# Causal attention loops: the first turned head of a pair right behind the value products, its copy ahead of the next exponentials

## The reference

```
even layer (here "fox", 8 heads):
    s = q k^T / 8 + (F_query - F_key)       # forget gate
    s = where(key <= query, s, -inf);  p = softmax(s);  o = p v
    beside it: a gated linear attention in chunks of 64 (here "GLA")
odd layer (here "odd", 16 heads):
    the top-k keys of an index score are kept; s = q k^T / 8 + bias(distance)
    s = where(kept and key <= query, s, -inf);  p = softmax(s);  o = p v
```

## Time and profile before

| | |
|---|---|
| median of 3 runs | 1404.54 us (1402.19 to 1405.95) |
| the profiled execution's own time | 1404.41 us |
| its span, first to last instruction | 1402.4 us |
| mean granted clock of TensorE, share of full speed | 0.993 |
| TensorE busy | 1361.1 us (97%) |
| VectorE, ScalarE, GpSimd busy | 971.0, 677.5, 72.4 us |
| fox loop, about | 631 to 672 us |
| odd loop, about | 1136 to 1194 us |

### The profile page before, as it was taken

How to read it: one execution, slowest core, us unless ns; L and a number is a source line. 1 busy time by engine, 2 the same in 40 slices (tenths; PEclk the granted TensorE clock), 3 DMA queues, 4 the chain that set the end, 5 groups by cost and what they waited for, 6 DMA issues and landing times.

```text
span 1402.4 us, 19395 instructions
## 1 busy us (share of the span) xinstructions
PE 1361.1 (97%) x7680; PEld 1156.9 (82%) x7680; DVE 971.0 (69%) x1321; ACT 677.5 (48%) x1056; POOL 72.4 (5%) x112
## 2 busy tenths in 40 slices
PE   8999999999999999998999999999999988999997
PEld 6888988888888888897888888888888866888886
DVE  5786776666687667657577667777666677576764
ACT  5576454443565444455554444444445455444442
POOL 0300010000000000003000000000000043000000
PEclk9999999999999999999999999999999999999999
DMA  8433556555446555454346555465554543465550
GB/s 301 156 125 121 180 173 219 180 184 191 165 155 217 190 195 176 160 177 147 122 150 216 196 188 180 157 204 186 191 187 148 163 137 88 150 210 189 181 191 34
DMA packets 67594, 241.31 MB, mean 172 GB/s; under 512 B 7999, under 2 KB 8392, under 8 KB 67504
## 3 DMA queue, kind: packets, MB, share of 16 engines
q1 hardware_dynamic: 65200, 234.19, 50.4%
q0 software_dynamic: 2016, 5.77, 1.6%
q10 hardware_dynamic: 288, 0.11, 0.0%
HBM read 238.88 MB, written 1.09 MB: 171 GB/s over the span
## 4 chain that ended last, share of the span: by engine, by line
PE 72%; issue 14%; DVE 6%; ACT 3%; DMA 2%; POOL 1%; DVEq 0%; POOLq 0%; ACTq 0%; SPq 0%
PE pp L455 71%; DVE wlo L1626 2%; PE pp L464 2%; DMA raw<-w_chunks 1%; ACT whi L1192 1%; DVE hx L1634 1%; DVE fa L1626 1%; ACT pbuf L1339 1%; DMA gns<-gains 0%; ACT hx L1193 0%; POOL fa L2346 0%; DVE fa L2173 0%; ACT xn L1231 0%; DVE fa L1634 0%; ACT fa L1193 0%
## 5 line engine op out<-in xcount | busy, mean ns | idle before, releaser
L455 PE MATMUL pp<-hx,whi 128*128 128x512 f32 (+1 forms) x2400 | 728.9, 365 | 6.0 <-DVE hx L1634 3.0
L1626 DVE TENSOR_TENSOR wlo<-raw,whi 128x1024 fp32r<-128x1024 f32 (+1 forms) x445 | 522.7, 1214 | 152.6 <-ACT whi L1192 152.3
L455 PE MATMUL pp<-hx,wlo 128*128 128x256 f32 x2032 | 569.3, 280 | 0.0
L455 PEld LDWEIGHTS pp<-hx,whi 128*128 128x128 f32 x2400 | 428.0, 189 | 89.0 <-issue 7.5
L1192 ACT ACTIVATE whi<-raw 128x1024 fp32r<-128x1024 f32 (+1 forms) x445 | 442.4, 1041 | 104.4 <-PE pp L455 93.6
L455 PEld LDWEIGHTS pp<-hx,wlo 128*128 128x128 f32 x2032 | 384.7, 189 | 2.1
L455 PE MATMUL pp<-whi,ra 128*128 128x512 f32 x1144 | 371.1, 395 | 0.0
L455 PEld LDWEIGHTS pp<-whi,ra 128*128 128x128 f32 x1144 | 215.2, 188 | 50.1 <-issue 0.9
L455 PE MATMUL pp<-wlo,ra 128*128 128x512 f32 x572 | 225.1, 394 | 0.0
L1706 DVE TENSOR_REDUCE fa<-pp 128x512 f32<-128x1024 f32 x104 | 126.9, 1220 | 80.8 <-PE pp L455 80.8
L1192 ACT ACTIVATE ra<-fa 128x512 fp32r<-128x512 f32 x63 | 39.8, 632 | 229.8 <-DVE fa L1634 229.8
(11 more groups left out here) (172 smaller groups left out, 775.4 us busy)
## 6 DMA issues: line engine op xcount, KB each, us to landing
raw<-w_chunks SPq DMA_DIRECT2D x437, 512.0 KB, 5.1
fa<-t_rows POOLq DMA_DIRECT2D x16, 128.0 KB, 3.4
raw<-w_chunks SPq DMA_DIRECT2D x5, 256.0 KB, 5.7
fx<-x_t SPq DMA_DIRECT2D x2, 512.0 KB, 5.1
X<-x_in SPq DMA_DIRECT2D x2, 512.0 KB, 9.2
fa<-g_fin POOLq DMA_DIRECT2D x2, 512.0 KB, 4.5
fa<-f_rows POOLq DMA_DIRECT2D x8, 128.0 KB, 3.2
out_dram<-X SPq DMA_DIRECT2D x2, 512.0 KB, 2.7
```

What stands on the lines that cost most here:

```text
L455: return pe.matmul(o, lhs, rhs, start=first, stop=last, skip_group_check=True)
L1626: return dve.tensor_tensor(o, a, b, op)
```

## The change

In the causal blocks, and only there, four orders are changed; every operation stays, and none is added.

- TensorE turns the first head of pair p-1 right behind the value products, ahead of `extra` and `fill(p, 0)`.
- ScalarE goes: copy of the first turned head, exponentials of the first head of pair p, copy of the second turned head, exponentials of the second head, the high part of pair p-2, `evict` of (p, 0), one split, `evict` of (p, 1) and (p, 2), one split. Where there is no pair p left, the split of (p, 0) stands between the two copies.
- VectorE takes the low part of pair p-2 and `evict` of (p, 0) behind the scaling of pair p, and `evict` of (p, 1) ahead of `lows(p, 0)`. Where there is no pair p left, `lows(p, 0)` stands ahead of `evict` of (p, 0).
- The rest is the same code put into functions (`high`, `low`, `exponentials`, `turned_copy`).

```diff
--- before.py
+++ after.py
@@ -686,12 +686,15 @@
                         weigh(2 * pr + 1, 0)
                         weigh(2 * pr, 1).then_inc(s_pv)
                         weigh(2 * pr + 1, 1).then_inc(s_pv)
+                    if causal and 1 <= p <= pairs:
+                        turn_weights(2 * p - 2)
                     point[0] = (p, 0)
                     extra(p)
                     fill(p, 0)
                     ended[name, p, 0] = consumed[0]
                     if 1 <= p <= pairs:
-                        turn_weights(2 * p - 2)
+                        if not causal:
+                            turn_weights(2 * p - 2)
                         fill(p, 1)
                         turn_weights(2 * p - 1)
                         fill(p, 2)
@@ -1317,37 +1320,61 @@
                         split_half()
                     split_at[name, p, at] = next_half[0]
 
+                def high(pr):
+                    act.wait_ge(s_pv, h0 + 2 * pr + 2)
+                    copy(out_hi(name, pr), ps[obk[pr % len(obk)]][:, 0:256]).then_inc(s_ohs)
+
+                def exponentials(h):
+                    hc = h0 + h
+                    nm, sm, rs = head_stats(hc)
+                    src = stt[:, h % 2, 0:tot] if causal else ps[sbk[h % 2]][:, 0:tot]
+                    if causal:
+                        act.wait_ge(s_smax, 2 * (hc - 16) + 2)
+                    else:
+                        act.wait_ge(s_negm, hc + 1)
+                    if h >= 4:
+                        act.wait_ge(s_ptn, hc - 3)
+                    if h >= 8:
+                        act.wait_ge(s_shr, hc - 7)
+                    o = weights_slot(name, h)
+                    for t in range(2):
+                        y = act.activation(o[:, off[t]:off[t] + kl[t]], src[:, off[t]:off[t] + kl[t]], ACT.Exp,
+                                           bias=nm[:, t:t + 1], scale=-1.0 if causal else 1.0, accum_out=sm[:, t:t + 1])
+                    y.then_inc(s_ex)
+
+                def turned_copy(h):
+                    act.wait_ge(s_ptn, h0 + h + 1)
+                    if h >= 2:
+                        act.wait_ge(s_pv, h0 + h - 1)
+                    copy(ptb[:, h % 2, 0:tot], ps[tbk[h % len(tbk)]][:, 0:tot]).then_inc(s_ptc)
+
                 for p in range(pairs + 2):
+                    if causal:
+                        for par in range(2):
+                            if 1 <= p <= pairs:
+                                turned_copy(2 * p - 2 + par)
+                            if p < pairs:
+                                exponentials(2 * p + par)
+                            elif par == 0:
+                                one_more(p, 0)
+                        if p >= 2:
+                            high(p - 2)
+                        evict((name, p, 0))
+                        if p < pairs:
+                            one_more(p, 0)
+                        evict((name, p, 1))
+                        evict((name, p, 2))
+                        one_more(p, 1)
+                        continue
                     if p >= 2:
-                        pr = p - 2
-                        act.wait_ge(s_pv, h0 + 2 * pr + 2)
-                        copy(out_hi(name, pr), ps[obk[pr % len(obk)]][:, 0:256]).then_inc(s_ohs)
+                        high(p - 2)
                     for h in (2 * p, 2 * p + 1) if p < pairs else ():
-                        hc = h0 + h
-                        nm, sm, rs = head_stats(hc)
-                        src = stt[:, h % 2, 0:tot] if causal else ps[sbk[h % 2]][:, 0:tot]
-                        if causal:
-                            act.wait_ge(s_smax, 2 * (hc - 16) + 2)
-                        else:
-                            act.wait_ge(s_negm, hc + 1)
-                        if h >= 4:
-                            act.wait_ge(s_ptn, hc - 3)
-                        if h >= 8:
-                            act.wait_ge(s_shr, hc - 7)
-                        o = weights_slot(name, h)
-                        for t in range(2):
-                            y = act.activation(o[:, off[t]:off[t] + kl[t]], src[:, off[t]:off[t] + kl[t]], ACT.Exp,
-                                               bias=nm[:, t:t + 1], scale=-1.0 if causal else 1.0, accum_out=sm[:, t:t + 1])
-                        y.then_inc(s_ex)
+                        exponentials(h)
                     evict((name, p, 0))
                     one_more(p, 0)
                     if 1 <= p <= pairs:
                         for par in range(2):
-                            h = 2 * p - 2 + par
-                            act.wait_ge(s_ptn, h0 + h + 1)
-                            if h >= 2:
-                                act.wait_ge(s_pv, h0 + h - 1)
-                            copy(ptb[:, par, 0:tot], ps[tbk[h % len(tbk)]][:, 0:tot]).then_inc(s_ptc)
+                            turned_copy(2 * p - 2 + par)
                             evict((name, p, 1 + par))
                     one_more(p, 1)
 
@@ -1798,6 +1825,11 @@
                     while next_half[0] < split_at.get((name, p, at), 0):
                         split_half()
 
+                def low(pr):
+                    dve.wait_ge(s_ohs, h0 // 2 + pr + 1)
+                    tt(out_lo(name, pr), ps[obk[pr % len(obk)]][:, 0:256], out_hi(name, pr).bitcast(F),
+                       ALU.subtract).then_inc(s_ols)
+
                 for p in range(pairs + 2):
                     for h in (2 * p, 2 * p + 1) if p < pairs else ():
                         hc = h0 + h
@@ -1820,13 +1852,11 @@
                                 dve.wait_ge(s_ex, hc - 7)
                             dve.tensor_reduce(nm, bank[:, 0:tot].rearrange("p (t k) -> p t k", t=2), AX.X, ALU.max,
                                               negate=True).then_inc(s_negm)
-                    if p >= 2:
-                        pr = p - 2
-                        dve.wait_ge(s_ohs, h0 // 2 + pr + 1)
-                        tt(out_lo(name, pr), ps[obk[pr % len(obk)]][:, 0:256], out_hi(name, pr).bitcast(F),
-                           ALU.subtract).then_inc(s_ols)
+                    if p >= 2 and not causal:
+                        low(p - 2)
                     lows(p - 1, 1)
-                    evict((name, p, 0))
+                    if not causal:
+                        evict((name, p, 0))
                     for h in (2 * p, 2 * p + 1) if p < pairs else ():
                         hc = h0 + h
                         nm, sm, rs = head_stats(hc)
@@ -1838,8 +1868,16 @@
                             sl = slice(off[t], off[t] + kl[t])
                             y = ts(o[:, sl], o[:, sl], rs[:, t:t + 1], None, ALU.mult, None)
                         y.then_inc(s_shr)
+                    if causal:
+                        if p >= pairs:
+                            lows(p, 0)
+                        evict((name, p, 0))
+                        evict((name, p, 1))
+                        if p >= 2:
+                            low(p - 2)
                     lows(p, 0)
-                    evict((name, p, 1))
+                    if not causal:
+                        evict((name, p, 1))
                     evict((name, p, 2))
```

## The result

| | before | changed kernel |
|---|---|---|
| median | 1405.24 us (1402.19 to 1406.85, 4 runs) | 1419.3 us (1417.31 to 1421.4, 4 runs) |
| ratio | | 1.0101 [1.0088, 1.0114] |
| profiled execution's span | 1402.4 us | 1419.4 us |
| fox, first scores to last value products | 39.04 us | 54.66 us |
| odd, the same | 55.36 us | 57.54 us |

The kernel is 1.0% slower, 14.1 us in the medians and 17.0 us in the two profiled spans. The profiled execution of the changed kernel is the slowest of its four (1421.4 us), that of the kernel before lies 0.8 us under its median, so sizes read from this pair of traces are on the high side. The 17.0 us by place: fox +15.6, odd +2.2, the stretches ahead of, between and behind the loops -0.8 together (the last one, from the last value products of odd to the end, took 210.75 against 210.74 us and takes nothing up).

The account below looks back on a forecast made before the run. TensorE, busy 97% of a 1402.4 us span, was taken as the bound. Fox +8.2 and odd +1.1 gave a span of 1411.7, and 2.0 more for the execution gave 1413.7 us; range 1406 to 1420.

Parts of the forecast that it names:

- What bounds the kernel, and that a loop's delay reaches its end: Whole kernel: TensorE busy 97% of 1402.4 us; delay at a loop's last value products reaches the end whole.
- The stall before go1: Fox, p = 4: the split ahead of the states makes TensorE wait 5.6 us; go1 starts 5.3 us later.
- Fox, p = 3: Fox up to p = 3: eviction and low behind the scaling delay the next value products by 1.65 us.
- the term taken at nothing: Both loops: VectorE's scalings meeting GpSimd's masks in the new order, bounded at -2 to +2 us, taken as 0.
- one fall of 1.8 among four places: Four short stalls, two in fox and two in odd: one clock fall of 1.8 us counted, booked on odd.
- Value products of p = 4 to go0's end: Fox, p = 4: value products, turn, extra(4) and three units take 4.15 us to go0's end.
- go1 to the last value products: Fox, end of the loop: this stretch takes 5.2 us instead of 4.06, +1.1.
- Odd: Odd loop: 0.7 us of gain left, one clock fall of 1.8 us, together +1.1 us.
- one fall behind the 5.6 us stall: Fox, behind the wait before go1: TensorE's clock falls once, +1.8 us.
- the rival with falls at all four short stalls: Fox and odd: three more clock falls of 1.8 us than counted, 1419.1 us; chance 0.12.
- the clock holds over short stalls: Fox and odd: only the 5.6 us stall brings a clock fall, +7.5 us, 1411.9 us; chance 0.12.
- Low is in time: Odd: VectorE does low before TensorE's next scores end, so the change wins, 1396 us; chance 0.09.

Follow-up runs that it names:

- e8: Kernel before, with only the split of (p, 0) put ahead of evict(p, 0) where no pair is left, on ScalarE and VectorE; 1409.81 us, ratio 1.0035.
- e9: Changed kernel plus unread identity products (9, 4, 11 and 23) filling TensorE's four stalls in fox; 1414.66 us, ratio 1.0059.
- e11: e4 with VectorE's low part behind both scalings in fox alone; 1398.64 us, ratio 0.9939.
- e7: e4 with the second turned head's copy put between the two exponentials; 1403.89 us, ratio 0.9992.
- e4: Changed kernel with only first turn and first copy early; second copy back behind exponentials and split, VectorE as before; 1397.4 us, ratio 0.9950.
- e10: e4's order in odd alone, fox as in the kernel before; 1399.03 us, ratio 0.9947.
- e6: e4 with VectorE's low part behind both scalings; 1398.48 us, ratio 0.9951.

## Why the prediction was right or wrong, point by point

The time, 1419.3, lies in the range given, 5.6 us above the forecast and 0.7 below the range's upper end. The direction and the mechanism came as forecast, the size did not: 9.2 us of loss were forecast and 14.1 measured. Span against span the forecast is 7.7 us too low: 7.4 in fox, 1.1 in odd, and 0.8 the other way in the other stretches. By its steps:

- *What bounds the kernel, and that a loop's delay reaches its end: right.* Nothing behind a loop took anything up (210.75 against 210.74 us).
- *The stall before go1: right to the tenth.* 5.6 forecast, 5.63 measured, with ScalarE's split ahead of the states as the rows above show; e8 has the same 5.6 in the old kernel.
- *Fox, p = 3: too small by 4.0.* Forecast +1.65 at p = 4's value products, measured +5.6. 1.1 of it is VectorE: extra(3) started at 653.43, and the loop had begun 0.98 us earlier than before, so that this stands against the forecast's 653.3 as 654.4. VectorE took 11.74 us before from its mask at 640.40 to kg's eviction at 652.14, and 12.64 us in the changed kernel (639.36 to 652.00), with the same instructions. So 0.9 of the 1.1 is the term taken at nothing, how VectorE meets GpSimd's masks; here are VectorE's and GpSimd's rows of the changed kernel:

```profile
644.47 2.10 DVE L1653 TENSOR_TENSOR wlo<-raw,whi 128x1024 fp32r<-128x1024 f32 x1
...
647.60 1.22 DVE L1653 TENSOR_TENSOR wlo<-raw,whi 128x1024 fp32r<-128x1024 f32 x1
...
648.93 1.03 DVE L1657 TENSOR_SCALAR pbuf<-pbuf,st 128x128 f32<-128x128 f32 x2
```

```profile
644.30 0.48 POOL L2349 TENSOR_TENSOR fa<-fa,cst 128x128 f32<-128x128 f32 x1
644.72 0.75 POOL L2350 TENSOR_TENSOR fa<-fa,cst 128x256 f32<-128x256 f32 x1
...
647.63 1.50 POOL L2349 TENSOR_TENSOR fa<-fa,cst 128x128 f32<-128x128 f32 x1 [2.15 <-DMA fa<-f_rows]
```

  A split of 1.22 us took 2.10 beside a mask, a mask of 0.48 us took 1.50 where a split had begun 0.03 us before it. The other 2.9 is the low clock over extra(3) and five units (from extra(3) to the next value products 11.54 us, against 8.71 in e9), where the forecast had one fall of 1.8 among four places.
- *Value products of p = 4 to go0's end: too small by 3.0.* 7.2 instead of 4.15, the second fall (extra(4) 3.70 instead of 1.99, units 0.64 instead of 0.36). The order of the work was right.
- *go1 to the last value products:* 7.4 against 5.2 and the counted 1.8, 0.4 too little.
- *Odd: about right, for partly wrong reasons.* Forecast +1.1, measured +2.2. The cycles measured 7.4, 5.6, 7.1, 6.4, 6.4 and 5.2 against 6.0, 5.3, 7.2, 6.4, 6.4 and 5.2. p = 3's value products came 1.2 late. The first cycle was 1.4 longer: the clock fell behind its wait as forecast (1.55 us for the eight products), but cost more than the 0.7 given to it there. The further fall of 1.8 that was counted did not come: the clock held over 2.45 and 1.96 us.

So the term that was mis-sized is the clock in fox. The prediction counted 1.8 us there, for one fall behind the 5.6 us stall, and 1.8 more for one of the four short stalls, which it booked on odd. Fox had two low stretches, and they lasted far longer than the one from which the 1.8 was read (granted clock 0.50 from 1161 to 1164 us in the kernel before): one from 653 to 659 us, and one from extra(4) through the 5.63 us stall to 683 us. By the rows the first was worth 2.8 us, the second 3.1 ahead of the stall and about 2 behind it, 7.9 in all. e9 gave back 7.9: 3.1 up to p = 4's value products, 2.7 from there to go1 and 2.1 behind it. The number came out at the rival with falls at all four short stalls (1419.1), but not by its places: the two in fox fell, the two in odd held. That the time lies inside the range is in part luck.

The other rivals: "the clock holds over short stalls" failed in fox. The Trainium skill (TensorE: Matmul & The Clock Gate, Part 1: The HAM clock gate), by which, as the prediction read it, the clock drops only after a whole window without work and shorter stalls are free, agrees with odd's 2.45 and 1.96 us. Falls behind 2.15 us (e11, below) and 2.81 us (e7), and in fox behind 2.28 and 0.98 us, disagree with that reading. "Low is in time" failed as reckoned: value products waited for the low part nine times. What the prediction missed there is that the gain of the earlier trace rows needs only the first copy early: e4 and e10 have it.

## What to carry to other kernels

Before a copy is put ahead of an engine's next work, ask what it waits for: the first turned head's copy waited for work already done and won 0.5%, while the second's waited for units still to run, and put the exponentials, the scaling and the evictions behind them on TensorE's chain. Where such a chain passes through an eviction for which TensorE waits, price the half clock behind its stalls with all the products that can follow in a low stretch (here up to 17 us of one), not with one typical fall. A split that needs the end of a product must not stand ahead of the evictions that the next product waits for: undoing that one order gave back 0.36%.

## What the runs showed of the hardware

The length of a wait did not decide whether TensorE's clock fell behind it. The same eight products after the same wait of 2.15 us, at the start of odd, in e10 and in e11:

```profile
1136.87 0.93 PE L455 MATMUL pp<-fa 64*128 64x128 f32 x8 [2.15 <-ACT fa L1195]
```

```profile
1136.65 1.65 PE L455 MATMUL pp<-fa 64*128 64x128 f32 x8 [2.15 <-ACT fa L1195]
```

```profile
652.64 2.08 PE L455 MATMUL pp<-fa 64*128 64x128 f32 x16 [0.98 <-DVE fa L1649]
```

```profile
652.34 1.16 PE L455 MATMUL pp<-fa 64*128 64x128 f32 x16 [0.98 <-DVE fa L1649]
```

e11 ran them at 1.2 GHz, e6 at 2.4. Every wait above 3 us in the two loops, from 3.33 to 5.63 us over all runs, had the low clock behind it. What decides between 1 and 2.8 us was not settled.

VectorE and GpSimd held each other up: a split took 2.10 instead of 1.22 us on one side, a mask 1.50 instead of 0.48 on the other. That is near the work that the other engine still had to do, 1.0 us of masks and 1.1 us of split, as if one waited for the other. The kernel before shows the same (a split of 2.02 us, masks of 1.72 instead of 0.73), so this is not new with the change, only 0.9 us more of it. By the Trainium skill (SBUF — State Buffer, SBUF: two separate sides) the two share a pair of ports under an exclusive lock, which a VectorE instruction with two SBUF inputs, as the split, needs against a GpSimd instruction that reads SBUF, and which goes to whichever starts first. The split at 647.60 that kept its 1.22 us while the mask begun at 647.63 took 1.50 agrees. The split at 644.47 began ahead of the mask at 644.72 but beside the one begun at 644.30, and was the one delayed, by 0.88 us, longer than the first mask's rest: the second mask seems to have gone ahead of it.

The best orders found here are those of e4 and e10, 0.5% faster than the kernel before and 1.5% faster than the changed one.
